# A two-layer streaming encoder: one activation table set for stick-breaking, and three masks moved into score products

## What is computed

```python
def _stick_breaking(q, k, v, q_pos, k_pos):
        z = einsum('bqhd,bkhd->bhqk', qb_, k) * SB_HD ** -0.5
        earlier = k_pos[None, :] < pb[:, None]
        log_fail = where(earlier, log_sigmoid(-z), 0.0)
        between = cumsum(log_fail, axis=3, reverse=True) - log_fail
        w = where(earlier, exp(log_sigmoid(z) + between), 0.0)
        return einsum('bhqk,bkhd->bqhd', w, v)

def _mla_attn(q_nope, q_rope, k_nope, k_rope, v, q_pos, k_pos):
        s = (q_nope . k_nope + q_rope . k_rope) * MLA_QD ** -0.5
        pr = softmax(where(k_pos // CHUNK <= q_pos // CHUNK, s, -inf))
        return einsum('bhqk,bkhd->bqhd', pr, v)
```

## Time and profile before

| | |
|---|---|
| median of 3 runs | 3257.71 us |
| profiled execution | 3269.8 us, its span 3268.0 us |
| TensorE matmul busy | 3016.0 us (92%) |
| ScalarE, VectorE, GpSimd busy | 1000.9, 837.2, 964.6 us (31, 26, 30%) |
| mean granted TensorE clock | 0.939 of full |
| chain that ended last | TensorE 80%, VectorE 8%, ScalarE 4%, issue 3%, GpSimd 3%, DMA 2% |
| stick-breaking | 694.6 to 918.9 us |
| latent attention, prompt heads | 2380.5 to 2533 us |

### The profile page before, as it was taken

How to read it: one execution, slowest core, us unless ns; L and a number is a source line. 1 busy time by engine, 2 the same in 40 slices (tenths; PEclk the granted TensorE clock), 3 DMA queues, 4 the chain that set the end, 5 groups by cost and what they waited for, 6 DMA issues and landing times.

```text
span 3268.0 us, 44316 instructions
## 1 busy us (share of the span) xinstructions
PE 3016.0 (92%) x17001; PEld 2648.2 (81%) x17001; DVE 837.2 (26%) x1822; ACT 1000.9 (31%) x2042; POOL 964.6 (30%) x888
## 2 busy tenths in 40 slices
PE   7999998988879799999888999988799989999988
PEld 7989987854668699899768989976666869989976
DVE  2111122123141421011333111132444342101143
ACT  3212223246332322122333212233444232212233
POOL 4433423320000334244243423323200034324323
PEclk9999998988786899999999999998789989999998
DMA  3322312320112132132122312221100113213212
GB/s 122 93 68 68 93 47 71 99 87 10 56 39 91 55 94 80 52 96 82 39 81 84 90 52 87 77 62 57 46 1 8 36 55 93 80 58 91 81 39 91
DMA packets 255388, 221.40 MB, mean 68 GB/s; under 512 B 15120, under 2 KB 200848, under 8 KB 255264
## 3 DMA queue, kind: packets, MB, share of 16 engines
q1 hardware_dynamic: 252432, 209.76, 20.9%
q10 hardware_dynamic: 2304, 8.39, 0.7%
q0 software_dynamic: 528, 1.64, 0.2%
HBM read 211.13 MB, written 8.60 MB: 67 GB/s over the span
## 4 chain that ended last, share of the span: by engine, by line
PE 80%; DVE 8%; ACT 4%; issue 3%; POOL 3%; DMA 2%; SPq 0%; ACTq 0%; DVEq 0%; POOLq 0%
PE ps L1531 22%; PE ps L1532 21%; PE ps L1533 21%; PE ps L1713 3%; PE ps L1739 3%; DVE y_rows L1213 2%; PE ps L1631 2%; DVE x_rows L1216 1%; DVE xt_lo L1231 1%; ACT silu_gate L741 1%; PE ps L1596 1%; DVE y_rows L1225 1%; PE ps L1649 1%; PE ps L1658 1%; POOL rs L1068 1%
## 5 line engine op out<-in xcount | busy, mean ns | idle before, releaser
L1531 PE MATMUL ps<-xt_hi,gu_hi 128*128 128x256 f32 (+1 forms) x2816 | 875.7, 311 | 24.2 <-DVE xt_lo L1231 18.3
L1532 PE MATMUL ps<-xt_lo,gu_hi 128*128 128x256 f32 (+1 forms) x2816 | 873.8, 310 | 0.0
L1533 PE MATMUL ps<-xt_hi,gu_lo 128*128 128x256 f32 (+1 forms) x2816 | 873.6, 310 | 0.0
L1054 POOL TENSOR_TENSOR ch_lo<-ch_raw,ch_hi 128x512 fp32r<-128x512 f32 (+2 forms) x324 | 403.0, 1261 | 1073.5 <-ACT ch_hi L703 1073.1
L1049 POOL TENSOR_TENSOR gu_lo<-gu_raw,gu_hi 128x512 fp32r<-128x512 f32 x352 | 455.2, 1296 | 730.0 <-ACT gu_hi L699 729.4
L1531 PEld LDWEIGHTS ps<-xt_hi,gu_hi 128*128 128x128 f32 x2816 | 538.1, 191 | 29.3 <-issue 17.6
L1532 PEld LDWEIGHTS ps<-xt_lo,gu_hi 128*128 128x128 f32 x2816 | 538.3, 191 | 0.0
L1533 PEld LDWEIGHTS ps<-xt_hi,gu_lo 128*128 128x128 f32 x2816 | 537.9, 191 | 0.0
L699 ACT ACTIVATE gu_hi<-gu_raw 128x512 fp32r<-128x512 f32 x352 | 222.7, 633 | 655.2 <-DMA gu_raw<-in_ffn_gu 654.8
L703 ACT ACTIVATE ch_hi<-ch_raw 128x512 fp32r<-128x512 f32 (+2 forms) x324 | 198.2, 620 | 559.3 <-DMA ch_raw<-in_ffn_dn 344.8
L1531 PE MATMUL ps<-ch_hi,ht_hi 128*128 128x512 f32 x880 | 343.4, 390 | 0.0
(11 more groups left out here) (231 smaller groups left out, 3238.2 us busy)
## 6 DMA issues: line engine op xcount, KB each, us to landing
gu_raw<-in_ffn_gu SPq DMA_DIRECT2D x352, 256.0 KB, 3.0
ch_raw<-in_ffn_dn SPq DMA_DIRECT2D x176, 256.0 KB, 3.5
ch_raw<-in_ab_in SPq DMA_DIRECT2D x48, 256.0 KB, 2.8
ch_raw<-in_ple_gate SPq DMA_DIRECT2D x32, 256.0 KB, 3.8
g_pre<-in_norms ACTq DMA_DIRECT2D x8, 512.0 KB, 4.8
g_post<-in_norms ACTq DMA_DIRECT2D x8, 512.0 KB, 3.8
ch_raw<-in_ab_out SPq DMA_DIRECT2D x16, 256.0 KB, 3.1
k_raw<-in_cache_sb_k SPq DMA_DIRECT2D x8, 512.0 KB, 3.8
```

Source lines behind the costliest of these rows:

```text
L1054: pool.tensor_tensor(ch_lo[:, c, 0:p["n"]], ch_raw[:, c, 0:p["n"]], ch_hi[:, c, 0:p["n"]].bitcast(F32), ALU.subtract).then_inc(ch_lo_ok, c ...
L1531: pe.matmul(out, a[0], b[0], start=start, stop=False)
L1532: pe.matmul(out, a[0], b[1], start=False, stop=False)
L1533: return pe.matmul(out, a[1], b[0], start=False, stop=stop)
```

## The change

1. Before stick-breaking, ScalarE loads the table set `natural_log_exp_and_others`, which holds Exp and Ln, and the loads between them go.
2. The two VectorE masks of stick-breaking (L1310, L1317) go. The mask constants become 0 or -2^100, and TensorE adds them to the scores by one more product per unit, identity times mask, float32r with 128 columns. VectorE makes the two float32r tiles before the first unit, and TensorE waits for them (`z_ok`). The clamp of w at 2.0 goes with its mask.
3. A prompt unit's scores take 128 rows in place of 64: the query comes from one of four tiles `q_one`, in which the 64 rows of the other head of its pair are zero. GpSimd fills them: four memsets and four copies (64x512) ahead of the output weights' low parts, and four more copies behind the samples' queries.
4. In latent attention the mask rides in the score product: rows 96 to 127 of `q_t` and `k_t` hold the rank-4 mask, loaded by three DMAs of SyncE's queue (1 MB to `q_t`, twice 128 KB to `k_t`) between the loads of the first and the second block of query weights. The product with `exact_masks` goes (64 times). `k_t` has two buffers and VectorE copies the rotary rows four times, not twice.
5. Keys are made for two heads at once (2 products with 128 weight and 512 data columns, 8 times in place of 16), and are issued three units ahead in place of one.

```diff
-    put("diag", k < q)
+    put("diag", np.where(k < q, 0.0, -BIG))
+        z_id = place("z_id", [P, P], F32R, SG.manual_sbuf_range[0] + 1024)
+        z_mask = place("z_mask", [P, 2 * P], F32R, r_y + 88064 + 4 * CONSTS["diag"][0])
-        k_t = place("k_t", [P, 2, PROMPT], F32, r_xt + 8192)
+        k_t = [place(f"k_t{i}", [P, 2, PROMPT], F32, o) for i, o in enumerate((r_xt + 8192, r_ch + KD * HALF * 4))]
...
-                            "z": [(slice(0, N), QKV["sb_k"][r, h // 2, kb * P:kb * P + P],
-                                   QKV["sb_q"][r, h // 2, kb * P:PROMPT])],
+                            "z": [(slice(0, N), QKV["sb_k"][:, h // 2, kb * P:kb * P + P], q_one[h % 4][:, kb * P:PROMPT]),
+                                  (slice(0, P), z_id[:], z_mask[:, 0:P])],
...
+                    z.append((slice(2 * P, 3 * P), z_id[:], z_mask[:, P + b * DEC_T:P + (b + 1) * DEC_T].unsqueeze(1).to_broadcast(
+                        [P, SB_HEADS, DEC_T])))
...
-                    preps.append({"i": len(preps), "kind": "head", "h": h, "unit": len(soft), "last": len(soft) + PT - 1})
+                        preps.append({"i": len(preps), "kind": "head", "h": h, "unit": len(soft), "last": len(soft) + 2 * PT - 1})
...
-                            "s": [(slice(0, P), slice(0, N), q_t[0:QD, h, qb * P:qb * P + P], k_t[0:QD, h % 2, 0:N], True),
-                                  (slice(0, P), slice(qb * P, N), exact("row_mask", P), exact("col_mask", P), False)],
+                            "s": [(slice(0, P), slice(0, N), q_t[:, h, qb * P:qb * P + P], k_t[h // 2 % 2][:, h % 2, 0:N], True)],
...
+        def prepared_at(units, n):
+
+            return [u for m in (1, 3) for u in units[n + m:n + m + 1] if u["prep"] and (u["prep"]["kind"] == "head") == (m == 3)]
...
+                    sp.wait_ge(y_mm, summed(ps[1]["i"], TILES - 1))
+                    for kt2 in k_t:
+                        sp.dma_start(kt2[QD:P], io["chunk_mask"][:, 1:2, :].to_broadcast([P - QD, 2, PROMPT])).then_inc(hm_in, 16)
+                    sp.wait_ge(v_ok, 2 * PT)
+                    sp.dma_start(q_t[QD:P, :, 0:PROMPT], io["chunk_mask"][:, 0:1, :].to_broadcast([P - QD, MLA_HEADS, PROMPT])
+                                 ).then_inc(hm_in, 16)
...
+                    act.preload_act_table_set("natural_log_exp_and_others")
...
-                        x, m = masked(u["sp"], u)
-                        dve.tensor_tensor(x, x, m, ALU.mult).then_inc(sb_spm, 1)
...
-                        dve.scalar_tensor_tensor(x, x, 2.0, m, ALU.min, ALU.mult).then_inc(sb_wm, 1)
...
+                    dve.tensor_copy(z_id[:], ident[:]).then_inc(z_ok, 1)
+                    dve.tensor_copy(z_mask[:], consts[:, CONSTS["diag"][0]:CONSTS["diag"][0] + 2 * P]).then_inc(z_ok, 1)
...
+                if kind == "head":
+                    pe.wait_ge(kt_ok, 2 * (i - 1))
+                    for c in range(2):
+                        mm = pe.matmul(PS[:, prep_bank(pr, i % 2), :], W_uk[:, c, pr["h"] * NOPE:(pr["h"] + 2) * NOPE],
+                                       lat_t[:, c, 0:PROMPT], start=c == 0, stop=c == 1)
+                    mm.then_inc(kt_tr, 2)
+                    return
...
-                        pe.wait_ge(sb_wm, i + 1)
+                        pe.wait_ge(sb_w, i + 1)
...
-                        pe.wait_ge(sb_spm, i + 1)
+                        pe.wait_ge(sb_sp, i + 1)
```

More of the change, by code:

```diff
@@ L115, in const_table, with chunk_mask_table @@
     put("batch_mask", np.where(np.arange(DEC_B)[:, None] == q // DEC_T, 0.0, -BIG), DEC_B)
+    return t
+def chunk_mask_table():
+    t = np.zeros((P - QD, 2, PROMPT), np.float32)
+    at = np.arange(PROMPT)
+    for r in range(PT):
+        t[r, 0] = np.where((at // P == r) & (at % P < P // 2), -BIG, 0.0)
+        t[r, 1] = (at // P == r) & (at % P >= P // 2)
     return t
@@ L199, in encoder @@
         lam_rows = place("lam_rows", [P, 4, HD], F32, SG.manual_sbuf_range[0] + 1024)
+        z_id = place("z_id", [P, P], F32R, SG.manual_sbuf_range[0] + 1024)
+        z_mask = place("z_mask", [P, 2 * P], F32R, r_y + 88064 + 4 * CONSTS["diag"][0])
+        hi_at = r_ch + CH * HALF * 4
+        q_one = [place(f"q_one{i}", [P, HALF], F32, o) for i, o in enumerate(
+            (r_ch + 10 * HALF * 4, hi_at + 8 * HALF * 4, hi_at + 9 * HALF * 4, hi_at + 10 * HALF * 4))]
         lam_cols = place("lam_cols", [P, 8], F32, SG.manual_sbuf_range[0] + 2048)
@@ L869, in soft_act @@
                                        bias=at_cols[:, i % 4, 0:1], accum_out=at_cols[:, i % 4, 1:2]).then_inc(at_exp, 1)
-                    if n + 1 < len(units) and units[n + 1]["prep"]:
-                        copy_kt(units[n + 1]["prep"])
+                    for u in prepared_at(units, n):
+                        copy_kt(u["prep"])
                     if n > 0:
@@ L1145, in _ @@
                                         "p h (b t) -> p h b t", b=DEC_B)).then_inc(qbd_ok, 1)
+                            pool.wait_ge(qbd_ok, 6)
+                            for h in range(4, SB_HEADS):
+                                one_head(h)
+                            pool.wait_ge(q_one_ok, 4 + SB_HEADS)
                             pad_queries()
@@ L1499, in _ @@
                     dve.wait_ge(mc_lat, 2 * TILES)
-                    for par in range(2):
-                        dve.tensor_copy(k_t[NOPE:QD, par, :], kr_t[NOPE:QD, 0:PROMPT]).then_inc(krt_cp, 1)
+                    for kt2 in k_t:
+                        for par in range(2):
+                            dve.tensor_copy(kt2[NOPE:QD, par, :], kr_t[NOPE:QD, 0:PROMPT]).then_inc(krt_cp, 1)
                     for g in range(4):
@@ L1590, in transpose_keys @@
                     pe.wait_ge(lat_in[pr["b"] % 3], 32 * (pr["b"] // 3 + 1))
+                if kind == "head":
[5 more added lines that the diff above has]
+                    return
                 for b in range(2):
                     if i >= 1:
-                        pe.wait_ge(kt_ok, 2 * (i - 1) + b + 1)
-                    if kind == "head":
-                        for c in range(2):
-                            mm = pe.matmul(PS[0:NOPE, prep_bank(pr, b), 0:256], W_uk[:, c, pr["h"] * NOPE:(pr["h"] + 1) * NOPE],
-                                           lat_t[:, c, b * 256:(b + 1) * 256], start=c == 0, stop=c == 1)
-                    elif kind == "latent" and b == 0:
+                        pe.wait_ge(kt_ok, 2 * i if kind == "latent" and pr["b"] == 0 else 2 * (i - 1) + b + 1)
+                    if kind == "latent" and b == 0:
                         for j in range(4):
@@ L1627, in scores @@
                         pe.wait_ge(qbd_ok, 6)
+                    else:
+                        pe.wait_ge(q_one_ok, 4 + u["head"] + 1)
                     if u["bank_before"] is not None:
@@ L1715, in soft_pe @@
                         mm.then_inc(at_s, 1)
-                    if n + 1 < L and units[n + 1]["prep"]:
-                        transpose_keys(units[n + 1]["prep"])
+                    for u in prepared_at(units, n):
+                        transpose_keys(u["prep"])
                     if 1 <= n <= L:
@@ L2028 @@
     arrays["in_consts"] = const_table()
+    arrays["in_chunk_mask"] = chunk_mask_table()
+    io["chunk_mask"] = nc.dram_tensor("in_chunk_mask", arrays["in_chunk_mask"].shape, _mybir.dt.float32, kind="ExternalInput").ap()
     io["consts"] = nc.dram_tensor("in_consts", arrays["in_consts"].shape, _mybir.dt.float32, kind="ExternalInput").ap()
```

49 lines of the change are left out of this document (28 added, 21 removed).

## The result

The changed kernel takes 3228.14 us (median of five runs, 3221.21 to 3235.47), the kernel before 3255.45 us beside it (3253.78 to 3265.77). The ratio is 0.9913, with a 95% interval of 0.9892 to 0.9933: 27 us faster, between 22 and 35. Measured a second time with other runs of both, the ratio was 0.9882 (0.9860 to 0.9904), 38 us. The profiled execution before took 3269.8 us, 14 above the median of these runs, so a difference of the two profiles (42.8 us of span) overstates the gain. I therefore use the profiles for where the time went, not for how much it is in all.

What follows compares the result with a forecast made beforehand. Waits through table loads and masks bound stick-breaking, TensorE alone latent attention. Gains of 21 + 19 + 1 + 1 - 1 = 41 us off the median 3257.7 gave 3217 us, range 3198 to 3243.

Steps and rivals of the forecast that it cites:

- The prompt part, 21 us: Stick-breaking prompt part: 97 us in place of 118, 21 us gained, between 10 and 27.
- my 11.4: Stick-breaking prompt: us per head with TensorE as the bound, 11.1 of its own work plus 0.3 for masks.
- scores over 128 rows in place of 64 stream the same columns; I cost them at nothing: Stick-breaking prompt scores: doubling the rows costs nothing, at worst the mask's price again.
- the low clock at the start: Start of the stick-breaking prompt part: some 10 us of work at half speed cost 5 us.
- The samples, 19 us: Stick-breaking samples: 81 us in place of 99.7, 19 us gained; 70 us without the low-clock term.
- If two samples' work (2 x 6 us) runs so, 11 us come on top: Stick-breaking samples: one slow stretch behind the pause for the last keys, at 1.93 times the time, adds 11 us.
- The second rival: Stick-breaking samples: the clock stays down, 100 to 128 us, whole kernel 3236 to 3264 us; chance 0.17.
- Latent attention, 1 us: Latent prompt heads: 1 us gained, between a loss of 4 and a gain of 17, as waits replace the keys' cover.
- the case without holes: Rival for latent attention: TensorE has no waits, so the stage gives 17 us, whole kernel 3201 us; chance 0.08.
- The mask's DMA, 1 us lost: Latent query weights: the 1 MB mask load may make a weight 0 to 5 us late; taken as 1.
- The end of the mixer, 1.3 us: Differential norm: one table load between Ln and Exp goes from the chain, 1.3 us gained.
- The slower rival: Latent attention: holes lower the clock, TensorE's work takes 245 us, whole kernel 3313 us; chance 0.04.

Runs made afterwards that it cites:

- experiment 1: Kernel before plus only the load of the table set with Exp and Ln ahead of stick-breaking; VectorE's masks stay: 3219.12 us, 0.9871 of the kernel before.
- Experiment 11: Changed kernel with stick-breaking prompt scores over a head's own 64 rows, without zero-filled queries, mask product kept: 3241.79 us, 0.9932 of the kernel before.
- Experiment 5: Changed kernel with the cached keys of the stick-breaking samples requested one sample earlier: 3224.81 us, 0.9875 of the kernel before.
- experiment 6: Changed kernel plus four unused products of 512 columns among the small score products of every stick-breaking sample: 3234.43 us, 0.9920 of the kernel before.
- Experiments 4 and 12: The runs keys_late and best, in this order: 3218.43 us and 3209.05 us.
- experiment 7: Changed kernel with the 1 MB latent mask load issued behind the next pass's weights instead of ahead of them: 3220.13 us, 0.9870 of the kernel before.
- Experiments 1, 2 and 10: The runs experiment 1, masks_only and tables_latent, in this order: 0.9871, 1.0032 and 0.9865 of the kernel before.
- latent_only: Kernel before with only the latent attention parts (mask rows, keys for two heads, three units ahead): 3263.59 us, 1.0002 of the kernel before.
- keys_late: Changed kernel with the latent keys of two heads issued one unit ahead in place of three: 3218.43 us, 0.9868 of the kernel before.
- after_again: Changed kernel measured once more without an edit: 3227.92 us, 0.9882 of the kernel before.
- best: tables_latent with stick-breaking samples' cached keys requested one sample earlier and latent pair keys in two halves, one per head: 3209.05 us, 0.9839 of the kernel before.
- tables_latent: Changed kernel with the stick-breaking masks back on VectorE, table set and latent part kept: 3222.43 us, 0.9865 of the kernel before.
- masks_only: Kernel before with only the stick-breaking masks joined to the scores, table loads left in: 3273.85 us, 1.0032 of the kernel before.

## Why the prediction was right and where it was wrong

The sign and the range were right: faster, 3228 us in 3198 to 3243. The number, 3217, was 11 us low, and two terms of its sum were far off and cancelled in part.

**The prompt part, 21 us: too small.** The direction was right and is shown by experiment 1: without the loads TensorE becomes the bound, and the chain is TensorE's throughout. The profiles gained 34 us (118.2 to 84.2). A head took 10.25 us in place of my 11.4, which makes 8 x 1.15 = 9 us. Without the masks a head took 10.87 us (experiment 1) where I had 11.1, which is 0.23 of the 1.15. The other 0.92 is the failed step, "scores over 128 rows in place of 64 stream the same columns; I cost them at nothing", with 0.08 us on top for the mask: these two were to add 0.3 us and took 0.62 away. I had read the 0.2 us that a score product takes beyond its columns as a start that every group pays. Experiment 11 shows that it goes with the step between tile shapes: over 128 rows, behind products of the same shape, 128 columns with the mask took 0.29 us, against 0.215 for the columns themselves. Some 2 us more are the low clock at the start, for which I counted 5 us: the clock was at 1.00 from 708 us on, not at 0.50 at 716 to 720 as in the earlier trace rows, and its mean of 0.96 over 84.2 us leaves 3. The casts lie ahead of the first clamp; they lasted 1.7 us in place of 0.7.

**The samples, 19 us: far too large.** Here I had named over 95 us as the bound beyond which I am wrong, and they took 95.4 and 95.5. The work was sized right: 62 us and 8 of waiting, and the window gives 95.4 x 0.71 = 68 us at full clock. The failed step is "If two samples' work (2 x 6 us) runs so, 11 us come on top". The clock took 27 us. In place of one low stretch there were five, which begin at about 787, 801, 808, 825 and 842 us. Four of them begin within 3 us of a gap in TensorE's work, the one at 801 us with TensorE busy since 787. Experiment 5 also refutes the reason: I had tied the low clock to the pause before the last keys, and with the pause gone the clock stayed at 0.70. By the same reckoning the samples before were 99.5 x 0.73 = 73 us of work, so the change took 5 us of work out, and that is what the stage gained. My sum set a term with a fifth of its work at the low clock against a measured one at 0.73. The second rival, that the clock stays down, was the nearer one in its mechanism; its 100 to 128 us assumed the low level throughout, and lie above what came.

The row from the differential samples in the earlier trace rows, a clock of 0.50 with TensorE busy all the time, was the better guide, and I gave it too little weight. The Trainium skill's rule in "TensorE: Matmul & The Clock Gate", section "What's actually happening", that activity releases the throttle, did not hold throughout in this case: the window at 848 us has TensorE busy 4.00 of 4.00 us at a clock of 0.50, and the added wide products of experiment 6 left the mean at 0.71. The differential samples show it for longer: TensorE was busy without a break from 951 to 1009 us, the clock stood at 1.00 until 961 us, and then at 0.50 to the end of the stretch. One window of it:

```profile
965.00:969.00 4.00, 4.00 (x21) 4.00 (x20) 0.00 (x0) 0.10 (x1) 0.00 (x0) 0.50 0.39 116
```

**Latent attention, 1 us: right, for the reason given.** A pair was forecast at 18.1 us, with 1.0 to 1.1 us of waiting per head, and took 18.10, with 0.37 + 0.58 = 0.95. The stage gained 1.9 us. Experiments 4 and 12 confirm the hole: moving the keys into it gives 5.8 us in the profile, moving halves 7.7. That is less than the 17 us of the case without holes: once the keys are late enough to fill them, the scores wait for ScalarE's copy.

**The mask's DMA, 1 us lost:** not shown either way. The stretch around it was 3 us longer in the profile, but 117.0 to 120.2 us among kernels with identical code there, and that difference is the clock's (experiment 7).

**The end of the mixer, 1.3 us: right in its place.** From the first product of the norm to the first product of the next stage it took 15.96 us before and 14.49 after. Up to the values matrix of latent attention nothing of it is left (1214.7 and 1214.5 us).

**The stick-breaking masks.** In the prediction they had little effect of their own: 0.3 us per head for the product, and the loss at the start. Experiments 1, 2 and 10 separate them: alone they cost 10 us, and beside the table set they give nothing (0.9865 without, 0.9882 with them). TensorE gains 0.6 us per head by them, 5 us in eight, and some 2 to 3 of these go to the later start.

**The slower rival** (holes lower the clock of latent attention) did not come: the clock there is 0.97 as before, with TensorE's busy share down from 145 of 149 us to 130 of 148.

Why the whole gain was 27 to 38 us, not 41 or more: the prompt part gave more than forecast and the samples' part almost nothing, and the profiled execution before lay above its median. It held 72.1 us of differential samples and 62.2 us of the pair ahead of them, where latent_only, with the same code there, took 67.5 and 60.7; that is 6 of its 14 us above the median.

## What to carry to other kernels

Two functions that alternate on ScalarE and lie on the chain are first brought into one table set: that one line gave the whole measured gain here, and the moves of masks onto TensorE gave none. Where products of different tile shapes alternate on TensorE, count the steps between shapes, and not only the columns. When work is taken away in front of a waiting engine, look at what it covered: a removed or merged step that had filled a hole gives its time back as waiting, and is better moved than removed. Never set a forecast at full clock against a measured stretch at a lower one; first divide both by the same clock, and treat the clock as a term of its own.

## What the runs showed of the hardware that was not expected

**The step between tile shapes costs time on TensorE.** Products of 64 rows between products of 128 rows take 0.2 us more than their columns (0.41 us for 128 columns, where further 128 columns add 0.21), and so does the 128-row triangle product behind the values with their 64 columns of the array (0.42 us). A product of 128 rows behind the 64-row scores takes 0.26 us more. Padding the queries with zeros to 128 rows took nearly all of it away (0.29 us for scores and mask). Doubling the rows with zeros made the scores faster.

**The same code runs at different clocks from one kernel to the next.** The differential samples, untouched by all edits, took 58.5 us at a granted clock of 0.74, 60.1 at 0.72, 61.5 at 0.70, 67.4 at 0.63 and 72.1 at 0.59. At full clock these are 42.5 to 43.3 us each time. The samples of stick-breaking took 84.9 us at 0.80 in keys_late and 95.5 at 0.71 in after_again, with the same instructions. What decides it was not found: the clock stayed low with the pause gone (experiment 5) and with wide products in between (experiment 6). In best the samples took 75.8 us at 0.86, for 65 us at full clock, and in tables_latent 92.1 at 0.70 for 64; but the prompt part, the same code in both, took 95.3 us at 0.85 in best and 89.8 at 0.92 in tables_latent. The low clock had in part moved to another stage. So the 16 us between their samples say little on the edit; the medians differ by 13 us and the ratios by 8, of which the latent heads are 7.

**A shorter pause is no surer clock.** In masks_only 0.30 us of VectorE's work left the chain of the head shown, and the head became 1.04 us longer, because 3 us of TensorE's work in it ran at 0.50.
